# Sums over later keys: from TensorE products to VectorE scans, with the weights turned by block transposes and a bounce through HBM

## The reference, cut to what matters

```python
for i in range(s // SB_QBLOCK):
    q0, q1 = i * SB_QBLOCK, (i + 1) * SB_QBLOCK
    z = jnp.einsum('bqhd,bkhd->bhqk', qf[:, q0:q1], kf[:, :q1])
    mask = (q0 + jnp.arange(SB_QBLOCK))[:, None] > jnp.arange(q1)[None, :]
    log_beta = jax.nn.log_sigmoid(z)
    log_keep = jnp.where(mask, jax.nn.log_sigmoid(-z), 0.0)
    later = lax.cumsum(log_keep, axis=3, reverse=True) - log_keep
    w = jnp.where(mask, jnp.exp(log_beta + later), 0.0)
    outs.append(jnp.einsum('bhqk,bkhd->bqhd', w, vf[:, :q1]))
```

## Time and profile before

| | us |
|---|---|
| median of 3 runs (lowest, highest) | 2084.54 (2084.04, 2084.89) |
| the profiled execution, its own time | 2085.62 |
| its span in the profile | 2083.8 |
| PE busy | 2076.4 |
| DVE busy | 1217.7 |
| ACT busy | 971.3 |
| POOL busy | 149.8 |

### The profile page before, as it was taken

The page is one execution under the profiler, slowest core; times in us unless marked ns, Lnnn a source line. Parts: engine busy times, 40 slices in busy tenths (PEclk is TensorE's granted clock), DMA queues, the critical chain, the costliest instruction groups (busy, mean ns, idle before and its releaser), DMA issues.

```text
span 2083.8 us, 22669 instructions
## 1 busy us (share of the span) xinstructions
PE 2076.4 (100%) x9420; PEld 1720.9 (83%) x9420; DVE 1217.7 (58%) x1298; ACT 971.3 (47%) x1084; POOL 149.8 (7%) x251
## 2 busy tenths in 40 slices
PE   9999999999999999999999999999999999999999
PEld 8878888888888888888888888888888888888887
DVE  7776655555455554656666666655555455554654
ACT  6565554443444434445455455554443444434443
POOL 1010100000000000011110100100000000000010
PEclk9999999999999999999999999999999999999999
DMA  9666766765667656678766666776765667666673
GB/s 332 216 203 193 248 216 219 234 209 196 194 212 235 209 200 189 212 236 250 227 216 206 208 195 202 237 216 220 236 206 198 192 212 237 207 201 188 212 237 130
DMA packets 214567, 447.37 MB, mean 215 GB/s; under 512 B 10225, under 2 KB 10241, under 8 KB 214209
## 3 DMA queue, kind: packets, MB, share of 16 engines
q1 hardware_dynamic: 197600, 392.72, 56.6%
q0 software_dynamic: 16448, 51.08, 9.3%
q10 hardware_dynamic: 416, 2.13, 0.3%
HBM read 419.67 MB, written 26.21 MB: 214 GB/s over the span
## 4 chain that ended last, share of the span: by engine, by line
PE 97%; DMA 1%; DVE 1%; issue 0%; SPq 0%; ACT 0%; POOL 0%; DVEq 0%; POOLq 0%
PE acc L1101 32%; PE acc L1102 32%; PE acc L1107 32%; DMA raw<-in_w_in 1%; DMA spread<-blocks 0%; DMA blocks<-folded 0%; PE turn_zb L1220 0%; DVE w_lo L746 0%; PE turn_zb L1121 0%; PE turn_zb L1193 0%; PE turn_zb L1131 0%; PE turn_zb L1160 0%; PE turn_zb L1133 0%; PE turn_zb L1132 0%; PE turn_zb L1211 0%
## 5 line engine op out<-in xcount | busy, mean ns | idle before, releaser
L543 ACT ACTIVATE w_hi<-raw 128x1024 fp32r<-128x1024 f32 x744 | 786.9, 1059 | 982.7 <-PE acc L1107 977.7
L746 DVE TENSOR_TENSOR w_lo<-raw,w_hi 128x1024 fp32r<-128x1024 f32 x744 | 899.8, 1221 | 579.2 <-ACT w_hi L543 578.8
L1101 PE MATMUL acc<-w_hi,xT_hi 128*128 128x512 f32 x2016 | 786.4, 390 | 1.7 <-DVE xT_lo L806 1.1
L1102 PE MATMUL acc<-w_hi,xT_lo 128*128 128x512 f32 x2016 | 784.5, 389 | 0.0
L1107 PE MATMUL acc<-w_lo,xT_hi 128*128 128x512 f32 x2016 | 538.8, 389 | 0.0
L1101 PEld LDWEIGHTS acc<-w_hi,xT_hi 128*128 128x128 f32 x2016 | 378.4, 188 | 81.5 <-DVE xT_lo L806 1.6
L1107 PEld LDWEIGHTS acc<-w_lo,xT_hi 128*128 128x128 f32 x2016 | 378.4, 188 | 78.7
L1102 PEld LDWEIGHTS acc<-w_hi,xT_lo 128*128 128x128 f32 x2016 | 378.4, 188 | 77.9
L1101 PE MATMUL acc<-w_hi,m_hi 128*128 128x512 f32 x956 | 372.4, 390 | 0.0
L1102 PE MATMUL acc<-w_hi,m_lo 128*128 128x512 f32 x956 | 371.9, 389 | 0.0
L1107 PE MATMUL acc<-w_lo,m_hi 128*128 128x512 f32 x956 | 255.5, 389 | 0.0
(11 more groups left out here) (155 smaller groups left out, 531.6 us busy)
## 6 DMA issues: line engine op xcount, KB each, us to landing
raw<-in_w_gate SPq DMA_DIRECT2D x88, 1024.0 KB, 5.2
raw<-in_w_up SPq DMA_DIRECT2D x88, 1024.0 KB, 6.0
raw<-in_w_down SPq DMA_DIRECT2D x88, 1024.0 KB, 5.1
raw<-in_w_qkv SPq DMA_DIRECT2D x48, 1024.0 KB, 5.6
raw<-in_w_out SPq DMA_DIRECT2D x32, 1024.0 KB, 5.1
raw<-in_w_in SPq DMA_DIRECT2D x26, 1024.0 KB, 5.5
blocks<-folded POOLq DMA_DIRECT2D x42, 512.0 KB, 4.0
spread<-blocks POOLq DMA_DIRECT2D x168, 128.0 KB, 5.9
```

What stands on the lines that cost most here:

```text
L543: nc.scalar.activation(w_hi[:, h.slot, :, :], raw[:, h.raw_slot, 2 * h.part:2 * h.part + 2, :], ACTF.Copy).then_inc(hi_ready, 1)
L746: nc.vector.tensor_tensor(w_lo[:, h.slot, :, :], raw[:, h.raw_slot, 2 * h.part:2 * h.part + 2, :], f32(w_hi[:, h.slot, :, :]), ALU.subtrac ...
L1101: nc.tensor.matmul(dst, hi[:, h.k0 + k, at], wh, start=h.opens and k == 0, stop=False)
L1102: nc.tensor.matmul(dst, lo[:, h.k0 + k, at], wh, start=False, stop=False)
```

## The change

- The logits get queries on partitions and keys along the row. So the tile of 128 is now q's (second tile) and the operand of 256 is k's.
- The sum over later keys is made by eight scans on DVE, backwards along each row of keys, in two slots; DVE subtracts it from z1 into `work`, and ACT's exp reads `work`. The products with `tri_r` and `ones_r` are gone, as are these masks and the split of soft(z); a mask `earlier_sb` is made in layer 0.
- The weights now lie with keys along the row and have to be turned: DVE folds them (three transposes of 128x512), POOL writes 768 KB to `w_blocks` and reads them back in four pieces to `w_spread`. POOL does this behind q1's, q2's and k3's bounces for groups 0 to 2, and ahead of the next phase's for group 3. ACT and DVE split the first key tile's weights from `w_spread`.
- The chunks have another order (`QKV`): the third iteration makes q2, k2, q3, the fourth k3, v2, v3. With that the slots are: z at 26, 48, 72, 88; fold of the weights at 35, 58, 82, 96; their split at 42, 65, 92, 103; the product with v at 44, 67, 95, 105.
- ACT, and no longer DVE, takes v of the second tile out of PSUM.

```diff
+QKV = [[("q", 0), ("k", 0), ("v", 0)], [("q", 1), ("k", 1), ("v", 1)], [("q", 2), ("k", 2), ("q", 3)], [("k", 3), ("v", 2), ("v", 3)]]
...
-    def z_at(self):
-        return self.fold_at(1) + Z_LAG
+    def split_at(self, c):
+        name, g = QKV[self.i][c]
+        return self.fold_at(c) + (FOLD_LAG if name == "q" and g < 3 else SHORT_LAG)
...
+QKV0 = next(ph for ph in PH if ph.name == "qkv").iterations
+Z_AT = [it.base - QKV0[0].base + it.fold_at(c) + Z_LAG for it in QKV0 for c in range(3) if QKV[it.i][c][0] == "k"]
+W_FOLD_AT = [Z_AT[0] + 9, Z_AT[1] + 10, Z_AT[2] + 10, Z_AT[3] + 8]
+W_SPLIT_AT = [Z_AT[0] + 16, Z_AT[1] + 17, Z_AT[2] + 20, Z_AT[3] + 15]
+PV_AT = [Z_AT[0] + 18, Z_AT[1] + 19, Z_AT[2] + 23, Z_AT[3] + 17]
+V_CHUNK = [(i, c) for i in range(4) for c in range(3) if QKV[i][c][0] == "v"]
...
+            def bounce_weights(g):
+                pool.wait_ge(w_fold_done, g + 1)
+                if g:
+                    pool.wait_ge(w_landed, 16 * QUARTERS * g)
+                pool.dma_start(w_blocks.rearrange("t p n -> p t n"), w_folded[:, :, :]).then_inc(w_out, 16)
+                pool.wait_ge(w_out, 16 * g + 16)
+                if g:
+                    pool.wait_ge(turned, QKV0[0].ph.turn(g - 1) + 1)
+                for b in range(QUARTERS):
+                    pool.dma_start(w_spread[b * BLK:(b + 1) * BLK].rearrange("j t a r -> j (t a) r"),
+                                   w_blocks[:, :, b * P:(b + 1) * P].rearrange("t (a j) r -> j (t a) r", a=QUARTERS)).then_inc(w_landed, 16)
+            qk0 = QKV0[0].ph.fold(0)
+            weights_follow = {qk0 + 2: 0, qk0 + 4: 1, qk0 + 7: 2}
             for F in range(len(FOLDS)):
+                if F == qk0 + 8:
+                    bounce_weights(3)
                 bounce(F)
+                if F in weights_follow:
+                    bounce_weights(weights_follow[F])
...
+                            for tt, v in enumerate((v1_hi, v1_2)):
+                                act.wait_ge(products_done, 2 * it.last_half(c) + tt + 1)
+                                nc.scalar.activation(v[:, :], acc[:, it.pair(c), tt, :], ACTF.Copy, scale=rstd[:, tt:tt + 1]).then_inc(v_rounded, 1)
+                    elif t == it.split_at(c):
+                        q = name == "q"
+                        F = ph.fold(2 * g + (not q))
                         act.wait_ge(fold_landed, 16 * QUARTERS * (F + 1))
...
-                if t == zt + 3:
-                    act.wait_ge(soft_ready, g + 1)
-                    nc.scalar.activation(part_hi[:, :], work[:, :], ACTF.Copy).then_inc(soft_rounded, 1)
-                if t == zt + 6:
-                    act.wait_ge(sum_done, g + 1)
-                    nc.scalar.activation(work[:, :], z1, ACTF.Exp).then_inc(w_exp, 1)
-                if t == zt + 7:
-                    act.wait_ge(w_ready, g + 1)
-                    nc.scalar.activation(part_hi[:, 0:8 * P], work[:, 0:8 * P], ACTF.Copy).then_inc(w_rounded, 1)
...
+                        split = slice(QUARTERS if q else 0, 2 * QUARTERS)
+                        nc.scalar.activation(by_tile((qT1_hi if q else kT1_hi)[:, :, :]), spread_tiles(F)[:, :, split], ACTF.Copy)
+                        nc.scalar.activation(by_tile((qT1_1 if q else kT1_1)[:, :, :]), spread_tiles(F)[:, :, 0:QUARTERS], ACTF.Copy).then_inc(qk_rounded, 1)
+            def qkv_groups(ph, t):
+                for g, zt in enumerate(Z_AT):
+                    if t == zt + 1:
+                        if g:
+                            act.wait_ge(w_fold_done, g)
+                        act.wait_ge(z_done, g + 1)
...
+                    if t == zt + 6:
+                        act.wait_ge(exponent_made, g + 1)
+                        nc.scalar.activation(work[:, :], work[:, :], ACTF.Exp).then_inc(w_exp, 1)
+                    if t == W_SPLIT_AT[g]:
+                        act.wait_ge(w_landed, 16 * QUARTERS * (g + 1))
+                        if g:
+                            act.wait_ge(turned, ph.turn(g - 1) + 1)
+                        nc.scalar.activation(by_heads(part_hi[:, :]), first_keys(), ACTF.Copy).then_inc(w_rounded, 1)
...
-                if t == zt + 3:
-                    dve.wait_ge(soft_rounded, g + 1)
-                    nc.vector.tensor_tensor(part_lo[:, :], work[:, :], f32(part_hi[:, :]), ALU.subtract).then_inc(soft_split, 1)
...
+                    if t in (zt + 3, zt + 4):
+                        dve.wait_ge(soft_ready, g + 1)
+                        rows = [slice(h * SEQ, (h + 1) * SEQ) for h in range(4)] + [slice((8 + h) * P, (9 + h) * P) for h in range(4)]
+                        for r in rows[0:3] if t == zt + 3 else rows[3:]:
+                            back = work[:, r][:, ::-1]
+                            ins = nc.vector.tensor_tensor_scan(back, ones_sb[:, 0:1].to_broadcast([P, r.stop - r.start]), back, 0.0,
+                                                               ALU.mult, ALU.add)
+                        ins.then_inc(soft_summed, 1)
+                    if t == zt + 5:
+                        dve.wait_ge(soft_summed, 2 * g + 2)
+                        nc.vector.tensor_tensor(work[:, :], z1, work[:, :], ALU.subtract).then_inc(exponent_made, 1)
+                    if t == zt + 7:
+                        dve.wait_ge(w_exp, g + 1)
+                        for d in diagonals(work[:, :]):
+                            ins = nc.vector.scalar_tensor_tensor(out=d, in0=d, scalar=1.0,
+                                                                 in1=earlier_sb[:, :].unsqueeze(1).to_broadcast([P, 4, P]),
+                                                                 op0=ALU.min, op1=ALU.mult)
+                        ins.then_inc(w_ready, 1)
+                    if t == W_FOLD_AT[g]:
+                        dve.wait_ge(w_ready, g + 1)
+                        if g:
+                            dve.wait_ge(w_out, 16 * g)
+                            dve.wait_ge(turned, ph.turn(g - 1) + 1)
+                        second = work[:, 0:8 * P].rearrange("p (k o b j) -> p o b k j", k=GRP, o=2, b=QUARTERS)
+                        first = work[:, 8 * P:].rearrange("p (k b j) -> p b k j", k=GRP, b=QUARTERS)
+                        for n, src in enumerate((first, second[:, 0], second[:, 1])):
+                            ins = nc.vector.transpose(w_folded[:, n, :].rearrange("p (b k t) -> p b k t", b=QUARTERS, k=GRP), src)
+                        ins.then_inc(w_fold_done, 1)
+                    if t == W_SPLIT_AT[g]:
+                        dve.wait_ge(w_rounded, g + 1)
+                        nc.vector.tensor_tensor(by_heads(part_lo[:, :]), first_keys(), f32(by_heads(part_hi[:, :])), ALU.subtract).then_inc(w_split, 1)
+                    if t == PV_AT[g] + 1:
+                        rows = slice(4 * g, 4 * g + 4)
+                        take_lo(ph.turn(g), [m_lo[:, rows, :].rearrange("p k t -> p (k t)")], [turn[:, :]],
+                                [m_hi[:, rows, :].rearrange("p k t -> p (k t)")])
...
-                if t == zt + 5:
-                    if g == 0:
-                        pe.wait_ge(masks_rounded, 1)
-                    pe.wait_ge(soft_split, g + 1)
-                    for x in (part_hi, part_lo):
-                        for at in range(0, 12 * P, CH):
-                            nc.tensor.matmul(z1[:, at:at + CH], tri_r[:, :], x[:, at:at + CH], start=False, stop=False, skip_group_check=True)
-                        for pair in range(2):
-                            first = z1[:, pair * CH:(pair + 1) * CH].rearrange("p (h q t) -> p h q t", h=2, q=2)
-                            second = x[:, 8 * P + pair * SEQ:8 * P + (pair + 1) * SEQ].rearrange("p (h t) -> p h t", h=2)
-                            ins = nc.tensor.matmul(first[:, :, 1, :], ones_r[:, :], second, start=False, stop=x is part_lo, skip_group_check=True)
-                    ins.then_inc(sum_done, 1)
...
+                    if t == zt:
+                        pe.wait_ge(qk_split, 2 * g + 2)
+                        if g:
+                            pe.wait_ge(exponent_made, g)
+                            pe.wait_ge(dve_took, ph.turn(min(g - 1, 1)) + 1)
+                        for h in range(4):
+                            at = h * SEQ
+                            three(z1[:, at:at + SEQ], (qT1_hi[:, h, :], qT1_lo[:, h, :]), (kT1_hi[:, h, :], kT1_lo[:, h, :]),
+                                  start=at % CH == 0, stop=h % 2 == 1, shared=True)
+                        for h in range(4):
+                            at = (8 + h) * P
+                            ins = nc.tensor.matmul(z1[:, at:at + P], qT1_1[:, h, :], kT1_1[:, h, :], start=h == 0, stop=h == 3, skip_group_check=True)
+                        ins.then_inc(z_done, 1)
+                    if t == PV_AT[g]:
+                        pe.wait_ge(w_split, g + 1)
+                        pe.wait_ge(acc_read, 2 * ph.chunk(*V_CHUNK[g]) + 2)
+                        pe.wait_ge(exponent_made, sum(z < t for z in Z_AT))
```

(39 more changed lines are left out.)

162 lines of the change are left out of this document (53 added, 109 removed).

## The result

| | before | after |
|---|---|---|
| median, us (lowest, highest, runs) | 2084.72 (2084.04, 2085.7, 6) | 2094.35 (2090.11, 2097.44, 6) |
| the profiled execution, its span | 2085.62, 2083.8 | 2095.26, 2093.2 |
| mean granted clock of PE in the span | 1.00 | 0.996 |

The ratio is 1.0043, 95% interval 1.0031 to 1.0054: 9.6 us slower, over twice what can be told from no change. The prediction said 2083.1.

The account below looks back on a forecast made before the run. PE, busy 2076.4 of 2083.8 us, was taken as the bound. Removed sums of 7.64 us against 6.25 us of new waits (0.45 + 1.7 + 4.1) gave -1.4 us: 2083.1, with 8 in 10 between 2077 and 2087.

Parts of the forecast that it names:

- The gain, 7.64 us: PE no longer makes the sums over later keys, 1.91 us in each of four groups; strided PV reads cost nothing.
- The scans, 3.6 us a group (2.8 to 4.4): Eight scans on DVE per group: 2.8 us lower bound, 4.4 if every element goes through twice, the middle taken.
- First logits, a wait of 0.45: Group 0's first z: k ready 0.95 us later with 0.51 in hand, so PE waits 0.45 us.
- product of group 0, a wait of 1.7: PE at group 0's PV: chain 34.4 us after slot 32 starts, PV at 32.7, so it waits 1.7 us.
- Group 1: 4.7 + 12.3 + 14.5 + 2.5 = 34.0: From slot 56's start: q2's fold 4.7, its bounce 12.3, the weights' bounce 14.5, rounding, subtraction and hand-overs 2.5 us.
- q2's bounce of 9.8 us: Time of q2's bounce in the trace before, 4.8 + 1.7 + 3.3 us; used for the lower bound and hidden case.
- the hidden case's 28.3: Group 1's chain if bounces land as q2's did: 4.7 + 9.8 + 11.3 + 2.5 us, PV at 29.9.
- The upper bound 16.6: Longest expected bounce of the weights, from k3's 14.1 us with the same added terms; 14.5 was taken.
- Fourth logits, "just covered": Group 3's z: k comes 0.95 us later with 1.06 in hand, so no wait; the scans may take that too.
- It waits 4.1 us ... no second loss follows: PE at group 1's PV, slot 67, waits 4.1 us; ACT and DVE have worked two slots ahead, so nothing more is lost.
- The one of bounces that collide with the loads: Rival: every bounce takes its upper bound, scans 4.4; waits 8.8, 6.4 and 0.45 us, +8.0 net, 2092.6; chance 0.11.
- The waits stay hidden: Rival: bounces land as q2's did, only the first z's 0.45 us wait is left; -7.2 us, 2077.3; chance 0.33.

Follow-up runs that it names:

- b1: The kernel before with half of the sums' products, those with `part_lo`, left out: 2081.53 us beside 2084.56, ratio 0.9987.
- e9: e5 with group 1's split of the weights one slot later and its product with v two slots later (66, 69): 2078.42 us, ratio 0.9967 to before.
- e5: The kernel after with the fold of the weights of groups 1 and 2 two slots later: 2081.89 us, ratio 0.9991 to before.
- e8: The kernel after with only group 1's fold of the weights two slots later (58 to 60): 2085.4 us, ratio 1.0 to before.
- e1: The kernel after with group 1's product with v 13 slots later, behind group 2's logits, its split at 71: 2087.4 us, ratio 1.0012 to before.
- e4: The kernel after with 39 extra 128x512 products on PE ahead of group 1's product with v: 2088.92 us, ratio 1.002 to before.
- a0: The kernel after once more, unchanged, as control on the second chip: 2096.77 us, ratio 1.0063 to before.
- e3: The kernel after with each scan shortened to 8 elements: 2091.5 us, ratio 1.0026 to before.
- e7: e6 with group 2's fold of the weights also two slots later (84): 2082.06 us, ratio 0.9983 to before.
- e2: The kernel after, POOL writing the weights without waiting for the landing of q's or k's read-back: 2088.2 us, ratio 1.0014 to before.
- e6: The kernel after with the edits of e1 and e2 joined, the latter for q1 and q2 only: 2080.95 us, ratio 0.9982 to before.

## Why the prediction was wrong, by its steps

- **The gain, 7.64 us:** right, by b1 and by e9. Products of v at full clock take 2.23 us, so the stride costs nothing, as said.
- **The scans, 3.6 us a group (2.8 to 4.4):** 3.8. The groups by shape:

```profile
L1080 DVE TENSOR_TENSOR_SCAN work<-ones_sb,work 128x256 f32<-128x256 f32 x16 | 10.1, 675 | 0.0
...
L1080 DVE TENSOR_TENSOR_SCAN work<-ones_sb,work 128x128 f32<-128x128 f32 x16 | 5.4, 399 | 0.0
```

  (675 - 399) / 128 = 2.16 ns an element, twice the 1.05 of a subtraction, and four of each are 4.3 us, less what neighbours overlap. The Trainium skill (DVE: opcode table, instruction layouts, handler registers and perf-mode slots, section Datapath and trigger behaviour) gives the scan half throughput; the trace agrees. It decided nothing: the fold of q2 ended 4.1 us after slot 56 starts (1150.05 - 1145.90), for 4.7.
- **First logits, a wait of 0.45; product of group 0, a wait of 1.7:** none in the profile after. k0's read-back landed sooner (ACT starts on it at 1052.48), and group 0's chain took 32.4 us for 34.4, its second bounce 12.5 (POOL 1093.44 to ACT 1105.94) for 14.5. Other runs show up to 2.2 at the first logits: such waits of a microsecond or two come and go with the loads.
- **"Group 1: 4.7 + 12.3 + 14.5 + 2.5 = 34.0": the step that failed, by size.** Measured 4.1 + 16.7 + 15.8 + 2.4 = 39.0; PE is at PV 30.1 us after the slot's start, so it waits 8.9 and not 4.1. The term that failed is the first bounce, 16.7 for 12.3; the second adds 1.3. The place, the order on POOL and the other two terms held. The first bounce was above even its upper bound of 14.1. It was taken from bounces of the trace before as if they were draws of one kind, but its length goes with where SyncE's next loads fall, and the change itself moves these through its transposes on DVE: with them two slots later (e5) the read-back in it is 3.9 us shorter and the write behind it 2.1. (The trace before had the hint: 5.8 us to the last landing for q2's read-back, with a load 2.0 us behind it, and 9.4 for k3's.) The prediction costed these at 2.1 us of a DVE with room, and did not ask what a `w_lo` 1.9 us later does to the loads.
- **Slips that leave the forecast as it is.** q2's bounce of 9.8 us took the median landing of its pieces (3.3) for that of the last, which was the slowest:

```profile
DMA to landing us min/median/max: 3.2/3.3/4.0
```

  So it is 10.6, and the hidden case's 28.3 is 29.9, with nothing in hand at PV. The upper bound 16.6 is 16.1 by the terms given (14.1 - 0.5 + 2.0 + 0.5). And in the kernel before, the logits of groups 0 and 1 stand 22 slots apart (at 26 and 48), not 24; slot 56 is named rightly.
- **Fourth logits, "just covered":** wrong in the same way. k3's read-back took 12.9 us, PE waits 3.6; it took 12.0 in e8, where group 2's transposes stay, and 7.9 in e5, where they move. e1 and e4 got 8.6 and 9.0 with the transposes in place, as the loads fell otherwise there. The 1.06 us in hand could not bear it. Groups 2 and 3 of the product with v were covered, as said.
- **"It waits 4.1 us ... no second loss follows":** wrong. PE itself is slower behind a wait. This is 5.4 us that the sum had no term for, and the trace of before, with no such wait in this phase, showed no price of it. Without it the kernel would still be slower than before, by about 4 us.
- **The rivals.** The one of bounces that collide with the loads came nearest, in its time (2092.6) and in what it names. Its mechanism was there in group 1 and at k3's bounce. That it forecast a wait of 8.8 in group 1, where 8.9 was measured, is luck in part: its terms were 5.5 + 14.1 + 16.6, the measured ones 4.1 + 16.7 + 15.8. So is the total: the 6.4 that it put on group 0 did not occur, and the fourth logits and the half clock stand in its place. "It must happen in all four" was wrong as a reason for its chance of 0.11: they were no independent draws. "The waits stay hidden" (2077.3) is what e9 is, once the transposes are moved.

**What stays open:** why load and read-back are both so much slower with one load 0.3 to 0.4 us behind the first of four reads and the next 3.4 to 5.1 behind it. That the place of the transposes sets the length of the read-back is shown by e5 and e8. That it does so through the loads is argued from the table: no run moved a load by itself. What the DMA engines do in these microseconds is not shown. The Trainium skill (DMA: Bandwidth & Descriptors, section Queues, rings and completion order) has each DMA engine take turns between the queues that have work for it, a packet at a time; with it both transfers would be slowed, as the rows above show, but it gives no reason for the difference of 4 us between +0.4 and -1.0.

## What to carry to other kernels

Work with room on its own engine can still be in the wrong place: ask which transfers its successor in the queue releases, and whether a chain of small transfers with a wait at each step begins just then. Moving three transposes by two slots, in two groups, was worth 11 to 15 us (e5 against the kernel after, and against a0 on the same chip), where their own duration is 1.9 a group. And a wait of TensorE of 1.8 us and more can cost above its length, since the work behind it may run at half the clock: 2.7 us for each of the two here, 1.6 to 3.0 over the runs.

## What the runs showed of the hardware

- TensorE's granted clock fell to 0.50 in every wait of 3.3 us and more in this phase. The waits of 3.3, 3.6, 3.8, 4.0, 8.9, 9.0 and 9.1 us were followed by a piece of 4.28 or 4.29 us for 2.25, the one of 6.0 (e1) by 3.74. What a wait costs behind it is half of the time at 0.50 that falls on work, and this isn't in step with the wait's length: 3.1 us and so 1.6 behind the wait of 6.0, 4.4 and so 2.2 behind that of 9.1 (e3), 5.4 and 2.7 behind that of 8.9, 6.1 and 3.0 behind that of 3.8 (e7); these prices are estimates from the granted clock.
- Waits of 1.8, 1.9, 2.0 and 2.7 us (e3, e2, e5, e8) had it too, with the fall 0.5 to 1.2 us behind the wait: pieces of 3.61, 3.88, 3.36 and 3.33. Behind waits of 0.4 to 1.6 us, and one of 2.2 (e6), the piece took 2.3. The Trainium skill (TensorE: Matmul & The Clock Gate, section What's actually happening) has the clock gated by how busy the engine has lately been; these rows agree. In e4, with work in the place of the wait, the clock stayed at 1.00.
- A scan costs 0.12 us and 2.16 ns an element, from the two shapes above.
- The same 512 KB read-back took about 8 or about 12 us, and with it went where two loads of 1 MB stood beside it.
